# Spreading a decoding query over the partitions by reads from device memory instead of TensorE and ScalarE

## The reference, cut to what matters

```
def moba_attention(q, k_all, v_all, q_start):
    ...
    kmean = jnp.mean(kb.astype(jnp.float32), axis=3)
    gate = jnp.einsum('bhqd,bhnd->bhqn', qh.astype(jnp.float32), kmean)   # picks key blocks
    ...
    s = jnp.einsum('bhqd,bhqnkd->bhqnk', q_c, kg) * scale
    p = jax.nn.softmax(s, axis=-1)
    o = jnp.einsum('bhqnk,bhqnkd->bhqd', p, vg)
```

## Time and profile before

| | us |
|---|---|
| median of 3 runs | 626.78 |
| lowest and highest run | 626.45, 630.81 |
| the profiled execution's own time | 624.19 |
| its span, first to last instruction | 622.3 |
| PE busy in it | 532.4 (86%) |
| DVE busy | 347.6 (56%) |
| ACT busy | 168.4 (27%) |
| POOL busy | 44.2 (7%) |

### The profile page before, as it was taken

The page is one execution under the profiler, slowest core; times in us unless marked ns, Lnnn a source line. Parts: engine busy times, 40 slices in busy tenths (PEclk is TensorE's granted clock), DMA queues, the critical chain, the costliest instruction groups (busy, mean ns, idle before and its releaser), DMA issues.

```text
span 622.3 us, 9565 instructions
## 1 busy us (share of the span) xinstructions
PE 532.4 (86%) x3597; PEld 423.2 (68%) x3597; DVE 347.6 (56%) x541; ACT 168.4 (27%) x235; POOL 44.2 (7%) x107
## 2 busy tenths in 40 slices
PE   4759899898999688784839967987999999999997
PEld 2428567575688466453405415966999999999997
DVE  1045275568788776845463256564646646644441
ACT  2310110631132122311000113435343443433331
POOL 7300000000104600000010100000000000000000
PEclk9868969988699879765865778999999999999999
DMA  6995428457049446616446999776564664555201
GB/s 204 300 350 197 125 79 270 129 139 240 0 143 324 151 133 205 206 65 203 135 139 220 322 342 336 234 235 193 181 186 157 201 194 151 181 186 185 71 19 35
DMA packets 99434, 114.63 MB, mean 184 GB/s; under 512 B 7343, under 2 KB 82240, under 8 KB 99372
## 3 DMA queue, kind: packets, MB, share of 16 engines
q1 hardware_dynamic: 93368, 104.46, 52.5%
q10 hardware_dynamic: 5188, 7.67, 3.7%
q0 software_dynamic: 832, 1.89, 0.8%
HBM read 111.20 MB, written 2.97 MB: 183 GB/s over the span
## 4 chain that ended last, share of the span: by engine, by line
PE 67%; DVE 19%; DMA 5%; ACT 4%; issue 3%; SPq 1%; ACTq 1%; DVEq 0%
PE bank L335 63%; DVE prod L896 3%; DVE s_all L992 3%; DVE mats L896 2%; DMA ring<-in_ada_w_dram 2%; DMA ring<-in_w_out_dram 2%; DVE cv L1100 1%; DVE BTP L896 1%; PE bank L504 1%; PE bank L351 1%; PE bank L380 1%; ACT w_part L1683 1%; DMA prod<-in_dn_norm_w_dram 1%; DVE w_ab L896 1%; ACT adaS L1515 0%
## 5 line engine op out<-in xcount | busy, mean ns | idle before, releaser
L335 PE MATMUL bank<-a_hi,w_part 128*128 128x264 f32 x832 | 154.8, 287 | 3.9 <-DVE a_lo L1437 2.1
L896 DVE TENSOR_TENSOR w_part<-ring,w_part 128x2048 fp32r<-128x2048 f32 (+1 forms) x38 | 84.9, 2236 | 89.5 <-ACT w_part L1683 89.5
L335 PEld LDWEIGHTS bank<-a_hi,w_part 128*128 128x128 f32 x832 | 130.9, 191 | 4.7 <-issue 2.6
L335 PE MATMUL bank<-a_lo,w_part 128*128 128x264 f32 x416 | 119.0, 286 | 0.0
L1683 ACT ACTIVATE w_part<-ring 128x2048 fp32r<-128x2048 f32 (+1 forms) x38 | 70.9, 1871 | 86.0 <-PE bank L335 76.2
L335 PE MATMUL bank<-hT,ring 128*128 128x264 f32 x352 | 88.5, 415 | 4.1 <-ACT proj L1538 2.1
L335 PEld LDWEIGHTS bank<-hT,ring 128*128 128x128 f32 x352 | 71.7, 206 | 21.1 <-issue 7.9
L335 PEld LDWEIGHTS bank<-a_lo,w_part 128*128 128x128 f32 x416 | 79.7, 192 | 0.1
L335 PE MATMUL bank<-hid_hi,w_part 128*128 128x264 f32 x352 | 64.9, 285 | 0.0
L335 PEld LDWEIGHTS bank<-hid_hi,w_part 128*128 128x128 f32 x352 | 54.5, 188 | 0.1
L335 PE MATMUL bank<-hid_lo,w_part 128*128 128x264 f32 x176 | 49.7, 282 | 0.0
(11 more groups left out here) (319 smaller groups left out, 588.1 us busy)
## 6 DMA issues: line engine op xcount, KB each, us to landing
ring<-in_ada_w_dram SPq DMA_DIRECT2D x24, 1024.0 KB, 7.4
ring<-in_cache_k_dram SPq DMA_DIRECT2D x64, 256.0 KB, 3.7
ring<-in_w_in_dram SPq DMA_DIRECT2D x11, 1024.0 KB, 5.8
ring<-in_w_gate_dram SPq DMA_DIRECT2D x11, 1024.0 KB, 5.3
ring<-in_w_up_dram SPq DMA_DIRECT2D x11, 1024.0 KB, 5.4
ring<-in_cache_v_dram SPq DMA_DIRECT2D x40, 256.0 KB, 3.8
ring<-in_w_down_dram SPq DMA_DIRECT2D x8, 1024.0 KB, 5.2
ring<-in_cache_v_dram ACTq DMA_DIRECT2D x24, 256.0 KB, 4.1
```

What stands on the lines that cost most here:

```text
L335: return pe.matmul(out, lhsT, rhs, start=start, stop=stop, skip_group_check=True)
L896: return v.tensor_tensor(out, a, b_, op)
```

## The change

The eight spreads leave PE and ACT. POOL writes the eight query rows once to a scratch tensor in device memory, waits until they have landed, and then for each sequence issues one DMA that reads the row of 2 KB for each of the 128 partitions into `qb`. DVE waits for that DMA, by one semaphore for each half of `qb`. The list `ORDER` still holds the names QB0 to QB7, but no engine has a part in them.

```
+        q_dram = nc.dram_tensor("q_rows_dram", [NS, AW], F32, kind="Internal").ap()
...
-            def q_spread(b_):                                    # PE
-                pe.wait_ge(sem("q_rows8"), 1)
-                b = opened(f"qb{b_}", 2)
-                closed(mm(b[:, :], ident[0:NS, b_:b_ + 1].to_broadcast([NS, P]), nat8[:, 0, :]), f"qb{b_}")
...
             def k_item(q, hf):                                   # DVE
                 slot = arrived(v, ("k", (q, hf)))
-                v.wait_ge(sem("qb"), q + 1)
+                v.wait_ge(sem(f"qb{q % 2}"), 16 * (q // 2 + 1))
...
-            def q_copy(q):                                       # ACT
-                b = full(a, f"qb{q}")
-                if q >= 2:
-                    a.wait_ge(sem("k_scored"), q - 1)
-                freed(a.activation(qb[:, q % 2, :], b[:, :], ACT.Copy), f"qb{q}")
-                a.wait_ge(bank_free[2], frees_at(f"qb{q}"))
-                a.sem_inc(sem("qb"), 1)
...
+            def spread_query(q):                                 # POOL
+                if q >= 2:
+                    g.wait_ge(sem("k_scored"), q - 1)
+                g.dma_start(qb[:, q % 2, :], q_dram[q, :].partition_broadcast(P)).then_inc(sem(f"qb{q % 2}"), 16)
+
+            g.wait_ge(sem("q_rows8"), 1)
+            g.dma_start(q_dram[:, :], nat8[:, 0, :]).then_inc(sem("q_stored"), 16)
+            g.wait_ge(sem("q_stored"), 16)
+            for q in range(4):
+                spread_query(q)
             g.wait_ge(sem("ebc"), 1)
             g.wait_ge(sem("qk_d"), 1)
             ...                                                  # the four products qdT
+            spread_query(4)
             g.wait_ge(sem("k_rows"), 2)
             ...                                                  # stores of keys and values
+            spread_query(5)
             ...                                                  # the prompt pooling
             g.sem_inc(sem("pool_prompt_done"), 1)
+            spread_query(6)
             g.wait_ge(sem("tails"), 3)
             ...                                                  # stores of the tails
+            spread_query(7)
             g.wait_ge(sem("max_diag"), 1)
```

More of the change, by code:

```diff
@@ L766, in _ @@
                 "DNORM": lambda _: head_spread("dn", "d_rec", 2, (4, 5, 6, 7)),
-                "QR": lambda _: to_rows8("q8", "q_done", QC0), "QB": q_spread,
+                "QR": lambda _: to_rows8("q8", "q_done", QC0),
                 "KR": lambda _: to_rows8("k8", "k_done", KC0),
@@ L1707, in _ @@
                 "KSUM": lambda _: head_root("kss", 1, 1.0 / HD, "rootk"), "DSUM": lambda _: head_root("dss", 2, 1.0, "rootd"),
-                "QB": q_copy, "KROW": k_rows, "VROW": v_rows, "TAILS": tails, "CONV": conv_gates, "AB": decays,
+                "KROW": k_rows, "VROW": v_rows, "TAILS": tails, "CONV": conv_gates, "AB": decays,
                 "GC": chunk_decays, "GBC": decay_matrices, "TI": dn_first, "L": dn_inner, "UA": dn_values,
```

## The result

| | before | changed |
|---|---|---|
| median, us (runs) | 627.83 (4) | 620.08 (4) |
| lowest to highest | 626.45 to 630.81 | 617.02 to 620.94 |
| span of the profiled execution | 622.3 | 615.2 |

The ratio is 0.9865, with a 95% interval from 0.982 to 0.991: 1.35% faster, 7.8 us by the medians. A second measurement gave 0.9863 (0.974 to 0.999). I had forecast 3.0 us and called a gain of more than 1% unlikely. The range held the time, but the forecast of "within 1%" was wrong: 4.8 us of gain are missing from my sum.

A forecast was written before the change was run, and what follows sets the result against it. At the first spreads PE was taken as late and DVE as early, idle 5.75 us before CEXT. Terms -0.75 - 1.1 - 1.0 - 0.1 = -3.0 us made a forecast median of 623.8 from 626.78, range 619.5 to 629.

The forecast's parts named there:

- Part 1: First row's store, read and wake-ups before K0: 8.0 us in all, K0 at 86.0, 5.0 us later.
- Parts 1 and 2 together: From K0 to CONV: PE starts W8 5.5 us earlier, K0's lateness is hidden, CONV at 100.9 against 101.66, gain 0.75.
- lateness of K0 less 5.75: Formula for CONV's shift: K0's lateness minus DVE's 5.75 us idle before CEXT; break-even with K0 at 86.7.
- The side cost: PE idles before W10, which starts at half clock for 7.5 to 11 us; counted as nothing, 1.4 us kept for the range.
- Part 3: Removing spreads QB2 to QB7 from PE: gains of 1.1 and 1.0 us, plus 0.1 for QB3, QB5 and QB7.
- QB4: Spread of row 4, in a stretch where PE has no gap: gain 1.1 us, at least 0.8.
- QB6: Spread of row 6, ending at 220.6 at half clock: gain taken as 1.0 us, between 1.0 and 2.1.
- QB2: Spread of row 2: no gain, since PE stands idle 2.06 us before W4, waiting for ACT.
- Part 4: Reads of rows 2 to 7 waiting in POOL's queue: none late, no loss counted for issues under a DVE multiply.
- the round trip is fast: Rival before K0: store 1.7, read 1.7 to 3.7 us, K0 at 82.4 to 84.4, total -6.5 to -4.5; chance 0.22.
- QB6's upper bound: Gain from row 6's spread if PE stays on the same clock, 2.1 us; takes the fast rival's total to -7.6.
- The bound on the whole: Whole kernel: change within about 1% (6.3 us) at 0.84, faster by more 0.10, slower by more 0.06.

The follow-up runs named there:

- rows 2 to 7 alone: Against the kernel before: only rows 2 to 7 go through memory, rows 0 and 1 still spread by PE and ACT; 622.01 us (4 runs), ratio 0.983.
- CEXT early: Changed kernel with the stage CEXT moved ahead of K0 in the order of all engines; 631.53 us (4 runs), no ratio given.
- ACT's queue: Changed kernel with the store and the reads of rows 0 and 1 issued by ACT instead of POOL; 624.03 us (one run).

## Why the prediction was wrong

By its own steps:

- **Part 1, the way through memory: a size that was off.** I took 3.1 for the store and 3.9 for the read and 0.5 for each wake-up, 8.0; they were 1.78, 3.43, 0.34 and 0.28, together 5.8, between my lower bound of 4.4 and the 8.0. The rows for small stores of 3.1 and 4.5 came from busy stretches; the 1.7 for 32 KB, taken at 317 us with the DMA engines 9 to 15% busy, was the right one. The shift of CONV was -2.65 in place of -0.75: this is 1.9 us of the missing 4.8. The rule of the Trainium skill ("DMA: Bandwidth & Descriptors", the anatomy of one DMA on the GpSimd path) would have done better: 2.0 and 2.6, an estimate that puts K0 at 83.6; it was at 84.36, with the copy 0.4 late. The trace agrees with it on the store (1.78), less on the read (3.43).
- **Parts 1 and 2 together: right.** PE early, DVE the bound, the formula "lateness of K0 less 5.75": with 2.97 it gives -2.78, measured -2.65. Four kernels with K0 elsewhere confirm the slope.
- **The side cost: mechanism right, size and sign wrong.** PE did idle (4.63 us) and W10 did start at half clock, but the clock was back after 3.3 us, not 7.5 to 11: W10 took 8.83, not 10.8 to 12.6. In the other traces with such a wait before W10 it took 8.79 to 10.10, and longest not behind the longest wait. And I followed it only to AB. I saw in the earlier trace rows that W4 waits for ACT and did not ask at which clock it ran; 9.04 us for 32 matmuls, against 7.39 for others of its kind, was in the trace. The later PE shortened its own wait ahead of W4, and W4 kept its clock: 1.7 us of gain in a place where the prediction had only a loss. This term was missing from the sum altogether.
- **Part 3: QB4 right in size (1.2 with rows 2 to 7 alone, 1.2 from K5 on in the changed kernel).** DVE's wait in M1 did not get shorter, as I had said it would (0.74 against 0.80): K7 and K8 had already taken the gain. **QB6 mis-sized.** I took 1.0, arguing that the clock comes back at a fixed moment. In the changed kernel it came back about 2 us earlier, beyond the lead that it had at K11, and 2.0 was saved at K12: 1.0 of the missing 4.8. With the 1.9 and the 1.7 that leaves 0.2. QB2 is nothing, as forecast.
- **Part 4: right.** No spread came late. K10 and K12 wait for no DMA. The 0.3 us of DVE at 194 us are the only sign of POOL holding it up. The eight reads add 2.1 MB, not 2.3.
- **The rivals.** What came is the rival "the round trip is fast" with QB6's upper bound, which I gave 0.22. It put the sum at -4.5 to -7.6; the span says -7.1. That the number fits is in part luck: with K0 where it came and QB6 in full, this rival's own terms make -6.1, and W4's clock, 1.7, was not among them. Its chance was too low because I weighed only landings. **The bound on the whole** failed as well: terms for the clock stood in the sum only as costs.

## What to carry to other kernels

When a stage moves, look at the clock of the matmuls behind the next wait: PE that arrives later at a wait may leave it faster, and one that arrives earlier may be slower than before (CEXT early). Price a transfer at a quiet moment by the shortest landing of its size, not by a middle one, and leave room: the same first read took 3.43 us in one kernel and 5.16 in another. And compare by milestones counted from the last instruction ahead of the edit: here they repeated to 0.6 us up to K15 where whole runs of one program differed by 13. They too can carry a draw of the clock, so a step of 1 or 2 us needs a second trace.

## What the runs showed of the hardware

- **A spread of the runs that the change does not touch.** From K15 to the softmax's reciprocal the 14 traces take either 42.3 to 43.2 us (seven of them, before and changed among them) or 49.1 (the other seven, the changed kernel again among them). The windows of 290 to 300 us show it, first in the changed kernel, then in the same program again:

```profile
290.00:295.00 5.00, 4.68 (x49) 2.31 (x47) 1.32 (x4) 0.25 (x1) 0.00 (x0) 1.00 0.01 4
295.00:300.00 5.00, 2.38 (x12) 1.53 (x13) 2.62 (x7) 0.35 (x1) 0.00 (x0) 1.00 0.76 231
```

```profile
290.00:295.00 5.00, 5.00 (x39) 2.24 (x38) 0.69 (x1) 0.00 (x0) 0.00 (x0) 0.50 0.00 0
295.00:300.00 5.00, 3.13 (x16) 1.47 (x8) 1.46 (x4) 0.60 (x1) 0.00 (x0) 0.50 0.85 234
```

  The clock rose in one before the ada columns and in the other behind them. That is 6.8 us, as much as the whole change. What decides it stays open. Behind the reciprocal the traces differ by another 7 us (297.4 to 304.4).
- **Transfers on POOL's queue.** A store of 16 KB landed in 1.78 us with the DMA engines quiet, against the 4.5 of the earlier trace rows; the eight reads of 256 KB took 3.4 to 6.2, median 4.5. With ACT's queue K0 came 1.1 us earlier: 0.6 in the two landings (1.46 and 3.13) and 0.5 in the wake-ups.
- **The port between DVE and POOL.** A POOL copy of 8 columns again took 2.21 us under K10's multiply; in the changed kernel no DMA issue on POOL took over 0.61.
